# Seven-product slots on two blocks of 144 tokens in place of 160 and 128

## What is computed

```python
z = h @ w_in                       # 1024 x 10240, columns split into u, v, q, k, vr, gr, ga, gb
u = gelu(u); v = layernorm(gelu(v))
a = u * mix_positions(v)           # masked 128 x 128 matrices, 8 groups
q = rotary(q); k = rotary(k) / 16  # 4 heads of 256
y, state = retention(q, k, vr, state0)     # 4 heads, vr 2048 wide
b = silu(gr) * groupnorm(y)
merged = sigmoid(ga) * (a @ w_a_out) + sigmoid(gb) * (b @ w_b_out)
x = x + gt1 * (merged @ w_o)
x = x + gt2 * moe(norm(x))         # 2 of 32 experts for each token
```

## Time and profile before

| | us |
|---|---|
| median of 3 runs | 1609.2 |
| lowest, highest | 1608.85, 1611.48 |
| span of the profiled execution | 1605.9 |
| TensorE (PE) busy | 1565.6 |
| VectorE (DVE) busy | 869.9 |
| ScalarE (ACT) busy | 275.5 |

### The profile page before, as it was taken

The page is one execution under the profiler, slowest core; times in us unless marked ns, Lnnn a source line. Parts: engine busy times, 40 slices in busy tenths (PEclk is TensorE's granted clock), DMA queues, the critical chain, the costliest instruction groups (busy, mean ns, idle before and its releaser), DMA issues.

```text
span 1605.9 us, 24827 instructions
## 1 busy us (share of the span) xinstructions
PE 1565.6 (97%) x9958; PEld 1080.8 (67%) x9958; DVE 869.9 (54%) x1812; ACT 275.5 (17%) x566; POOL 57.2 (4%) x103
## 2 busy tenths in 40 slices
PE   6999999999999999999999999999999998999997
PEld 3899888765698544444459999886649965444443
DVE  2676764565753454334457768556475434434436
ACT  3210000112200431111131100011121033111111
POOL 0000000001001100000000000000010001000000
PEclk9999999999999999999999999999999999999999
DMA  9734575488943799999983446535896438999993
GB/s 397 299 133 158 218 281 235 158 346 336 416 147 132 284 393 421 421 421 421 423 344 139 155 156 265 207 114 238 329 395 252 158 119 332 422 421 421 422 421 143
DMA packets 49810, 461.41 MB, mean 287 GB/s; under 512 B 5968, under 2 KB 6224, under 8 KB 10144
## 3 DMA queue, kind: packets, MB, share of 16 engines
q1 hardware_dynamic: 44656, 414.38, 64.5%
q10 hardware_dynamic: 3456, 37.75, 5.6%
q0 software_dynamic: 1584, 7.69, 1.2%
HBM read 415.88 MB, written 43.91 MB: 286 GB/s over the span
## 4 chain that ended last, share of the span: by engine, by line
PE 86%; issue 7%; DMA 3%; DVE 2%; ACT 1%; POOL 1%; DVEq 0%; SPq 0%; POOLq 0%; ACTq 0%
PE ps L795 86%; DMA state_sample_out<-ring 1%; DMA ring<-stream 1%; ACT work L1255 1%; DMA ovd<-sorted_rows 0%; DVE rope L1577 0%; DMA sorted_rows<-work,packed_rows 0%; DVEq L1521 0%; DMA cst<-consts 0%; POOL sorted_rows L761 0%; POOL kzm L741 0%; POOL rstd L709 0%; DVE hT L2129 0%; DVE hT L1595 0%; ACT L1255 0%
## 5 line engine op out<-in xcount | busy, mean ns | idle before, releaser
L795 PE MATMUL ps<-ring,work 128*64 128x512 f32 x1536 | 339.3, 595 | 2.8 <-ACT work L1255 2.8
L795 PEld LDWEIGHTS ps<-ring,work 128*64 128x64 f32 x1536 | 113.3, 137 | 211.2 <-issue 209.4
L795 PE MATMUL ps<-work,ring 128*128 128x160 f32 (+2 forms) x1600 | 231.4, 307 | 0.0
L1255 ACT ACTIVATE work<-ps 128x256 f32<-128x256 f32 (+5 forms) x238 | 102.3, 444 | 741.8 <-PE ps L795 733.2
L795 PEld LDWEIGHTS ps<-work,ring 128*128 128x128 f32 x1600 | 217.4, 191 | 13.4
L795 PE MATMUL ps<-ring,hT 128*32 128x128 f32 (+2 forms) x1776 | 171.4, 313 | 5.0 <-ACT hT L1255 5.0
L795 PE MATMUL ps<-hT,ring 128*128 128x160 f32 (+2 forms) x1024 | 169.7, 320 | 0.8 <-DMA ring<-stream 0.8
L795 PEld LDWEIGHTS ps<-hT,ring 128*128 128x128 f32 x1024 | 149.3, 191 | 17.7 <-issue 2.9
L795 PEld LDWEIGHTS ps<-ring,hT 128*32 128x32 f32 (+1 forms) x1776 | 126.8, 132 | 42.9 <-issue 29.3
L795 PE MATMUL ps<-work 128*128 128x288 f32 (+3 forms) x608 | 152.1, 393 | 3.4 <-DVE hT L2103 2.6
L795 PEld LDWEIGHTS ps<-work 128*128 128x128 f32 (+1 forms) x608 | 100.7, 185 | 53.9 <-issue 26.9
(11 more groups left out here) (222 smaller groups left out, 1169.6 us busy)
## 6 DMA issues: line engine op xcount, KB each, us to landing
ring<-stream SPq DMA_DIRECT2D x194, 1024.0 KB, 10.8
ring<-stream SPq DMA_DIRECT2D x95, 2048.0 KB, 8.9
state_sample_out<-ring ACTq DMA_DIRECT2D x16, 2048.0 KB, 9.1
state_out<-prm ACTq DMA_DIRECT2D x8, 512.0 KB
work<-sorted_rows SPq DMA_DIRECT2D x6, 512.0 KB, 5.1
prm<-params SPq DMA_DIRECT2D x1, 2608.5 KB, 27.7
prm<-params POOLq DMA_DIRECT2D x1, 2608.5 KB, 16.6
cst<-consts SPq DMA_DIRECT2D x1, 1651.0 KB, 21.0
```

What stands on the lines that cost most here:

```text
L795: return nc.tensor.matmul(out, lhsT, rhs, start=start, stop=stop, **k)
L1255: return act.activation(out, in_, func, **k)
```

## The change

Feature-major slots cut the 288 tokens in two blocks of 144 (`RIDE` = 144, `RIGHT` = 144 to 288, `LEFT` = 0 to 144), so all seven products are 144 wide. The sums of u, b and, for feature-major slots, of h are four arrays of equal width with no copied columns. Token-major slots keep their 128 + 128 + 32 tokens and get sums of their own: `sums_t` in `ovd`, 128 wide, made in ("v", 0) as before; `sums_h`, 144 wide, is made in step ("v", 1) behind the turned weights and ahead of the join, and lies in `work` behind `SG_AT`. `sums_u` moves into the region of q and k. `sums_ready` counts four a layer. `first`, `upper` and `lower` in the join have one width.

```diff
-RIDE = P + NS
+RIDE = TOK // 2
...
-        def sums_of(flat, half):
-
-            at = [0, half * RIDE, 2 * half * RIDE, 2 * half * RIDE + half * P]
...
-        sums_h = sums_of(ovd[:, :], KT // 2)
-        sums_u = sums_of(work[:, SG_AT + 512:SG_AT + 512 + KT * TOK], KT // 2)
-        sums_b = sums_of(work[:, SG_AT:SG_AT + 2 * KT * TOK], KT)
+        def sums_of(flat, half, width):
+            return [cut(flat[:, n * half * width:(n + 1) * half * width], half, width) for n in range(4)]
+
+        sums_t = sums_of(ovd[:, :], KT // 2, P)
+        sums_h = sums_of(work[:, SG_AT + KT * TOK:SG_AT + 2 * KT * TOK], KT // 2, RIDE)
+        sums_u = sums_of(work[:, QK_AT + 12 * RIDE:QK_AT + 12 * RIDE + KT * TOK], KT // 2, RIDE)
+        sums_b = sums_of(work[:, SG_AT:SG_AT + 2 * KT * TOK], KT, RIDE)
...
-        RIGHT, LEFT = slice(P, TOK), slice(0, P)
+        RIGHT, LEFT = slice(RIDE, TOK), slice(0, RIDE)
...
# token_seven
-                s1, s4, s2, s3 = sums_h
+                s1, s4, s2, s3 = sums_t
...
-                pe.wait_ge(sums_ready, 3 * l + 1)
+                pe.wait_ge(sums_ready, 4 * l + 1)
...
# feature_seven
-                    out, width = out_of(l, step, name), tokens.shape[2]
+                    out = out_of(l, step, name)
                     for c in range(part.shape[2] // P):
                         for k in range(half):
-                            last = mm(out[:, c, 0:width], part[:, k, c * P:c * P + P], tokens[:, k, :],
+                            last = mm(out[:, c, :], part[:, k, c * P:c * P + P], tokens[:, k, :],
...
-                        feature_seven(l, step, hT, sums_h, 1)
+                        feature_seven(l, step, hT, sums_h, 2)
...
# token_sums
+                left, right = slice(0, width), slice(width, 2 * width)
+                a11, a12, a21, a22 = act[:, 0:half, right], act[:, half:2 * half, right], act[:, 0:half, left], act[:, half:2 * half, left]
                 settle()
-                dve.tensor_tensor(s1[:, :, 0:P], a21, a22, ALU.add)
-                dve.tensor_tensor(s3, a11[:, :, 0:P], a21, ALU.subtract)
-                dve.tensor_copy(s1[:, :, P:RIDE], a11[:, :, P:RIDE])
-                dve.tensor_copy(s4[:, :, P:RIDE], a12[:, :, P:RIDE])
-                settle()
-                dve.tensor_tensor(s2, s1[:, :, 0:P], a11[:, :, 0:P], ALU.subtract)
-                settle()
-                dve.tensor_tensor(s4[:, :, 0:P], a12[:, :, 0:P], s2, ALU.subtract).then_inc(sums_ready, 1)
+                dve.tensor_tensor(s1, a21, a22, ALU.add)
+                dve.tensor_tensor(s3, a11, a21, ALU.subtract)
+                settle()
+                dve.tensor_tensor(s2, s1, a11, ALU.subtract)
+                settle()
+                dve.tensor_tensor(s4, a12, s2, ALU.subtract).then_inc(sums_ready, 1)
...
# join: the same for m7, c22 and m4
-                taken(dve.tensor_tensor(first[:, :, 0:P], first[:, :, 0:P], out_of(l, step, "m6")[:, :, 0:P], ALU.add), (l, step, "m6"))
+                taken(dve.tensor_tensor(first, first, out_of(l, step, "m6"), ALU.add), (l, step, "m6"))
...
# VectorE's steps ("v", 0) and ("v", 1)
-                        token_sums(hT, sums_h)
+                        token_sums(hT, sums_t)
...
                         turn_weights(l, step)
+                        token_sums(hT, sums_h)
                         join(l, step, *parts_of(step)[1:])
```

More of the change, by code:

```diff
@@ L429, in build @@
         kz_late = cut(prm[:, ln_at:ln_at + D], 2, 2, DK)
-        def sums_of(flat, half):
-            at = [0, half * RIDE, 2 * half * RIDE, 2 * half * RIDE + half * P]
-            return (cut(flat[:, at[0]:at[0] + half * RIDE], half, RIDE), cut(flat[:, at[1]:at[1] + half * RIDE], half, RIDE),
-                    cut(flat[:, at[2]:at[2] + half * P], half, P), cut(flat[:, at[3]:at[3] + half * P], half, P))
-        sums_h = sums_of(ovd[:, :], KT // 2)
-        sums_u = sums_of(work[:, SG_AT + 512:SG_AT + 512 + KT * TOK], KT // 2)
-        sums_b = sums_of(work[:, SG_AT:SG_AT + 2 * KT * TOK], KT)
+        def sums_of(flat, half, width):
[4 more added lines that the diff above has]
+        sums_b = sums_of(work[:, SG_AT:SG_AT + 2 * KT * TOK], KT, RIDE)
         rope_flat = rope.rearrange("p a t -> p (a t)")
@@ L449, in partial @@
             if kind == "b":
-                return cut(vrs[:, 0:RIDE], 1, RIDE), cut(vrs[:, RIDE:2 * RIDE], 1, RIDE), cut(vrs[:, 2 * RIDE:2 * RIDE + P], 1, P)
+                return [cut(vrs[:, n * RIDE:(n + 1) * RIDE], 1, RIDE) for n in range(3)]
             at, width = SG_AT if kind in ("q", "k", "vr") else QK_AT, P if kind in ("v", "vr") else RIDE
-            return W(at, 2, width), W(at + 2 * RIDE, 2, width), W(at + 4 * RIDE, 2, P)
+            return [W(at + 2 * n * RIDE, 2, width) for n in range(3)]
         def quarters(step):
             if step[0] == "b":
-                return cut(kzm_flat[:, 0:RIDE], 1, RIDE), cut(kzm_flat[:, RIDE:RIDE + P], 1, P), cut(kzm_flat[:, RIDE + P:RIDE + 2 * P], 1, P)
+                return [cut(kzm_flat[:, n * RIDE:(n + 1) * RIDE], 1, RIDE) for n in range(3)]
             at = (SG_AT if step[0] in ("q", "k") else QK_AT) + 6 * RIDE
-            return W(at, 2, RIDE), W(at + 2 * RIDE, 2, P), W(at + 4 * RIDE, 2, P)
+            return [W(at + 2 * n * RIDE, 2, RIDE) for n in range(3)]
         def turned():
@@ L865, in product @@
                     for k in range(KT // 2):
-                        last = mm(out[:, 0:2 * P], tokens[:, k, 0:P], part[:, k, :], fresh and k == 0, k == KT // 2 - 1, skip_group_check=True)
+                        last = mm(out[:, 0:2 * P], tokens[:, k, :], part[:, k, :], fresh and k == 0, k == KT // 2 - 1, skip_group_check=True)
                     made(last, (l, step, name))
-                product("m1", hT[:, 0:KT // 2, RIGHT], 0, 0)
-                pe.wait_ge(sums_ready, 3 * l + 1)
+                product("m1", hT[:, 0:KT // 2, P:2 * P], 0, 0)
+                pe.wait_ge(sums_ready, 4 * l + 1)
                 product("m3", s4, 1, 1)
-                product("c11", hT[:, KT // 2:KT, RIGHT], 1, 0, False)
+                product("c11", hT[:, KT // 2:KT, P:2 * P], 1, 0, False)
                 pe.wait_ge(weights_ready, 4 * n + 1)
@@ L879, in token_seven @@
                 pe.wait_ge(weights_ready, 4 * n + 4)
-                product("m4", hT[:, KT // 2:KT, LEFT], 1, 0)
+                product("m4", hT[:, KT // 2:KT, 0:P], 1, 0)
             def feature_seven(l, step, act, sums, sums_n):
@@ L899, in feature_seven @@
                 product("m1", act[:, 0:half, RIGHT], 0, 0)
-                pe.wait_ge(sums_ready, 3 * l + sums_n)
+                pe.wait_ge(sums_ready, 4 * l + sums_n)
                 product("m3", s4, 1, 1)
@@ L985, in _ @@
                         wait_reads(pe, [(l, (m, n), "t") for m in ("mix", "mixs") for n in range(4)])
-                        feature_seven(l, step, uT, sums_u, 2)
+                        feature_seven(l, step, uT, sums_u, 3)
                     elif kind == "b":
@@ L989, in _ @@
                             wait_reads(pe, [(l, ("bts", 0), "t")] + [(l, ("bt", n), "t") for n in range(8)])
-                        feature_seven(l, step, bT, sums_b, 3)
+                        feature_seven(l, step, bT, sums_b, 4)
                     elif kind == "o":
@@ L1597, in token_sums @@
             def token_sums(act, sums):
-                half = act.shape[1] // 2
+                half, width = act.shape[1] // 2, sums[0].shape[2]
                 s1, s4, s2, s3 = sums
-                a11, a12, a21, a22 = act[:, 0:half, RIGHT], act[:, half:2 * half, RIGHT], act[:, 0:half, LEFT], act[:, half:2 * half, LEFT]
+                left, right = slice(0, width), slice(width, 2 * width)
+                a11, a12, a21, a22 = act[:, 0:half, right], act[:, half:2 * half, right], act[:, 0:half, left], act[:, half:2 * half, left]
                 settle()
-                dve.tensor_tensor(s1[:, :, 0:P], a21, a22, ALU.add)
-                dve.tensor_tensor(s3, a11[:, :, 0:P], a21, ALU.subtract)
-                dve.tensor_copy(s1[:, :, P:RIDE], a11[:, :, P:RIDE])
-                dve.tensor_copy(s4[:, :, P:RIDE], a12[:, :, P:RIDE])
+                dve.tensor_tensor(s1, a21, a22, ALU.add)
+                dve.tensor_tensor(s3, a11, a21, ALU.subtract)
                 settle()
-                dve.tensor_tensor(s2, s1[:, :, 0:P], a11[:, :, 0:P], ALU.subtract)
+                dve.tensor_tensor(s2, s1, a11, ALU.subtract)
                 settle()
-                dve.tensor_tensor(s4[:, :, 0:P], a12[:, :, 0:P], s2, ALU.subtract).then_inc(sums_ready, 1)
+                dve.tensor_tensor(s4, a12, s2, ALU.subtract).then_inc(sums_ready, 1)
             def turn_first(l, step):
@@ L1647, in join @@
                 wait_made(dve, (l, step, "m7"))
-                taken(dve.tensor_tensor(lower, first[:, :, 0:P], out_of(l, step, "m7")[:, :, 0:P], ALU.add), (l, step, "m7"))
```

(5 more changed lines are left out.)

## The result

| | before, us | after, us |
|---|---|---|
| median (lowest to highest) | 1609.03 (1607.63 to 1611.48), 4 runs | 1598.78 (1598.39 to 1600.17), 4 runs |
| span of the profiled execution | 1605.9 | 1596.8 |
| PE busy | 1565.6 | 1554.6 |
| DVE busy | 869.9 | 877.2 |

The ratio on record is 0.9943, 95% interval 0.9931 to 0.9955. It is not the quotient of the two medians, which is 0.9936: by the ratio the change is worth 9.2 us, by the medians 10.3, by the two profiled spans 9.0. The forecast was 1600.5, a ratio of 0.9946 to its 1609.2.

The account below looks back on a forecast made before the run. TensorE, one queue of matmuls busy 1565.6 of 1605.9 us, was taken as the bound. 1605.9 - 9.0 (slots) + 0.2 (stall) + 0.1 (wider join) = 1597.2; with 3.3 from span to median, 1600.5 us; range 1598.8 to 1605.4.

Parts of the forecast that it names:

- The price of 144: Changed slots on PE: a 144-token record costs 122.6 ns, a slot 13.73 us for 14.05, 9.0 us over 28 slots.
- the two bounds: Cost of a 144-token record: 122.6 ns if 128 sits on a floor, 123.7 if its excess fades evenly to 160.
- Rival (a): Matmuls of changed slots: excess fades with width, 123.7 ns a record, gain 5.5 us less 0.3, 1604.0 us; chance 0.13.
- The surplus over the columns: Per changed slot: fewer columns explain 0.21 of the 0.32 us; the rest is 48 records leaving the floor.
- The first rule cited: Isolated matmul: streaming time plus about 2.5 ns at any width; 128 columns then take 109.2 ns, gain only 6.0 us.
- Rival (d): Changed slots: columns taken in blocks of 32, so 144 costs as much as 160; 33 us slower, 1642; chance 0.05.
- The late sums: New DVE sums in ("v", 1), 3.1 us: join starts 1.55 us late, 0.25 reaches ("u", 0), no PE stall.
- The cover that was named: Join of ("v", 1): its own waits for m7 and m4 absorb the delay from the new sums, all but 0.25 us.
- rival (c): New sums delay ("u", 0) by their whole 3.1 us: PE loses 2.6 us a layer, 5.2 in two, 1605.7; chance 0.07.
- ("ga", 1): Slot behind the mixing steps: in layer 0 PE stalls 0.2 us for the first turned weight; no second stall in layer 1.
- Rival (b): Layer 0's gain ahead of the state steps, 3.2 us, swallowed by a DMA-anchored wait for the stream: 1603.7; chance 0.09.
- The term mis-sized: Distance from profiled span to median: 3.3 us before, kept unchanged to get 1600.5 from a span of 1597.2.

Follow-up runs that it names:

- widths run: Changed kernel with 136 more matmuls, 96 to 256 wide with 128, 64 or 32 stationary columns, in layer 0's filler step; its one time 1628.15 us.
- doubled sums: Changed kernel with the 144-wide sums of h made twice, one behind the other, in step v1; 1605.28 us, ratio 0.9983.

## Why the prediction was right

- The price of 144. The choice between the two bounds was made on one fact, that 160 lies on the line of 256 and 288 to a tenth, and was right: 122.5 measured, 122.6 taken, and the widths run shows the edge at which the floor ends. Rival (a), the fading excess, is excluded: by it 136 would lie above 116.5, and it measures 115.9.
- The surplus over the columns. 256 columns fewer in a slot are 0.21 us; the slot lost 0.33. The other 0.12 is 48 records leaving the floor. The first rule cited ("Back-to-back issue gap" in the Trainium skill's "TensorE: Matmul & The Clock Gate"), an isolated matmul's 2.5 ns beside the streaming, fails at 128 with 128 stationary columns (112 ns) and holds with 64 or 32 (109); the section says itself that in a stream this rule comes out too low for narrow matmuls. Its warning that load and matmul set the spacing together is borne out, here in the form of a maximum. The 106.7 ns for 128 columns, worked out from the rule of the section "LDWEIGHTS (loading the stationary operand)", stand 5 ns below the floor of 111.7 measured.
- Rival (d), blocks of 32 columns, is excluded: 132, 136 and 140 each have a price of their own.
- The late sums. 0.25 us was to reach ("u", 0), and 0.16 did: the turned weight for m6 ended 7.54 us into the slot (7.38 before), PE asked at 7.84. The sums took 3.0 us. The cover that was named (the waits for m7 and m4) is the one that took them, as the doubled sums show: take it away and they cost their full length. That is rival (c), whose condition did not hold; its price for sums in PE's way whole, 2.6 us a layer, is near what the second 3.1 us of sums cost (3.0).
- ("ga", 1): a stall of 0.2 us expected, 0.19 measured, of which 0.09 is PE waiting; none in layer 1, as taken. The two together are a coincidence in part: the prediction counted only the wait for the weight, and the slower second record was not in it.
- Rival (b), the gain swallowed in the state steps: the chain moved with PE. The store starts at 384.28 in place of 387.76, 3.5 us sooner, the load at 399.19 in place of 403.35, and PE waits 0.6 instead of 0.8 behind it. This is one profile each: in the other profiles of kernels with the twenty slots of u, ga, a, q and k changed that wait is 0.9 to 1.4. So some tenths of the gain may be lost there, but not the 3.2 us of the rival.
- The term mis-sized is what lies around the span. 3.3 us were taken, the distance of one profiled span to the median of other executions. Later runs list time and span for each execution, 77 in all: the distance is 1.5 to 2.1 us in 63 of them and 2.7 to 3.2 in the other 14 (10 of these are of the kernel before, and none is of the changed kernel). The executions of the result have 1.6 to 1.8 (1598.6 with a span of 1596.8). The span was forecast as 1597.2 and came out as 1596.8, so of the 1.7 us by which the forecast missed some 1.5 are this term. What decides between the two distances is not known; that the median still rounds to the edge of the range is luck.
- A term left out: near its end the changed kernel waits 0.9 us for the weight stream, which the kernel before does not (last section). The sum had nothing for it. The 28 slots gave 9.3 in place of the 9.0 of the forecast, and other stretches differ by some tenths between profiles, so part of the closeness of the span is luck too.

## What to carry to other kernels

An uneven split of a width costs more than its columns when the narrow part lies on the floor that goes with the stationary columns (here 111.7 ns a record with 128 of them, at the full clock): fit a line through the wide matmuls' start distances and see which narrow ones lie above it. Read the price of a matmul from the distance of starts, never from the duration in a group row. For work added to an engine with idle time, look at what that engine waits for next: an addition ahead of two waits for a producer is free up to their sum, here about 1.5 us of late start with 0.2 us passed on, and then costs in full.

## What the runs showed that was not expected

- The start of the program differs by 2 to 3 us between executions of like kernels, and most of it goes with the granted clock. From 24 to 32 us that was 0.79 in the profile of before, 0.84 in that of after, and 1.00 with the doubled sums: a piece of the window at 1.2 GHz and the rest at 2.4, or all of it at 2.4. ("v", 1) then starts at 49.41, 49.02 and 47.05. It is not all of it, since two other profiles with 1.00 there have 46.50 and 47.59. PE is busy throughout that window in all three:

```profile
24.00:32.00 8.00, 8.00 (x27) 2.80 (x26) 0.00 (x0) 0.97 (x2) 0.00 (x0) 0.79 1.01 430
```

That is before; this is with the doubled sums (columns as in the windows above):

```profile
24.00:32.00 8.00, 8.00 (x37) 2.66 (x39) 0.00 (x0) 0.60 (x1) 0.00 (x0) 1.00 1.01 423
```

The same happens in the routing steps ahead of the experts. There the stretches of the table carry it: in layer 0 the kernel before had a piece at 1.2 GHz and the changed one had none (before, then after),

```profile
560.00:570.00 10.00, 6.89 (x44) 6.11 (x44) 8.39 (x24) 3.60 (x8) 0.00 (x0) 0.83 1.00 343
560.00:570.00 10.00, 7.45 (x48) 3.89 (x48) 8.48 (x27) 5.72 (x12) 0.00 (x0) 1.00 1.01 367
```

and in layer 1 both had one. In its second profile the changed kernel had the piece in layer 0 too, and that stretch took 350.46 us in place of 349.84. The stretches from ("v", 1) to ("vr", 0) are free of it in every profile. What makes the clock fall in one execution and not in the next was not tried. It is likely a part of the scatter of a single time (1605.1 to 1611.5 for the kernel before), and a comparison of two spans carries it.
- Beside a long operation of GpSimd (POOL in the rows) an addition on VectorE can take twice its time: the last of the 128-token sums in layer 1 takes 1.43 us in the changed kernel, where 0.69 is usual.

```profile
823.14 0.69 DVE L1603 TENSOR_TENSOR ovd<-hT 128x512 f32<-128x512 f32 x1
...
824.07 1.55 POOL L718 TENSOR_SCALAR_AFFINE_SELECT prm<-prm 128x1024 f32<-128x1024 f32 x1
824.73 1.43 DVE L1607 TENSOR_TENSOR ovd<-hT,ovd 128x512 f32<-128x512 f32 x1
```

The same two overlap in the trace of before, and there the addition keeps its 0.69:

```profile
830.06 0.69 DVE L1610 TENSOR_TENSOR ovd<-hT,ovd 128x512 f32<-128x512 f32 x1
830.11 1.60 POOL L720 TENSOR_SCALAR_AFFINE_SELECT prm<-prm 128x1024 f32<-128x1024 f32 x1
```

What differs is who starts first. With the addition ahead by 0.04 or 0.05 us it takes 0.69, in the profiles of before and of five of the runs; with GpSimd's operation ahead by 0.66, in the changed kernel and in the widths run, it takes 1.43 and ends 0.54 us behind that one's end. With the sums made early, GpSimd's operation starts at 825.15 for 1.60 us, and an addition of 576 that starts at 825.89 takes 1.47 in place of 0.76, ending 0.61 behind it. That fits an addition held back until GpSimd is done; no run was made to test it. DVE has idle time there, and nobody waits.
- PE waited 0.9 us for the weight stream near the end of the experts of layer 1 in the changed kernel, and not before. It is there in all six profiles of kernels with the twenty slots of u, ga, a, q and k changed, and absent in before and with b alone changed. From the experts of layer 1 to the end the two kernels without it take 256.44 and 256.30 us, five with it 256.84 to 257.46. So it is a price of the change, of some half a microsecond to one. What causes it was not tried.
